# A one-core decoder layer with gathered experts: front stages in other slots, eight mixer weight buffers, and the v gather ahead of the u gather

## The chip, the cores and the metric
The kernel runs on one NeuronCore of one Trainium2 chip. The metric is the device time of one execution in microseconds (us); lower is better. Before the change it is 3838.55 us, the median of three runs (3834.42 to 3840.43).

## The reference, cut to what matters
One layer over 1024 tokens of width 1024, all in float32:

```python
z = rms_norm(h) @ w_in                       # 14 tiles RWKV-7, 8 tiles convolution, 16 tiles of gates, 128 columns each
o_r = rwkv7_branch(...)                      # recurrence over tokens, 8 heads of 64, then @ w_o (512 -> 1024)
o_c = conformer_conv_branch(...)             # 31 taps on 512 channels, layer norm, silu, then @ w_o (512 -> 1024)
h = h + (g_r * o_r + g_c * o_c) @ w_out      # sigmoid gates
# product-key experts: 8 heads x 16 experts per token = 128 rows of u_tab and of v_tab per token
...
        u = jnp.take(u_tab, ib, axis=0)
        coef = gb * jax.nn.gelu(jnp.einsum('cd,ced->ce', xb, u), approximate=False)
        return jnp.einsum('ce,ced->cd', coef, jnp.take(v_tab, ib, axis=0))
...
h = h + ple_gate * (p[i] @ ple_w_proj[i]); return rms_norm(h, final_norm_g)
```

Each token needs 128 rows of 4 KB from each of the two tables, so that the kernel gathers 1.07 GB.

## The kernel before, in words
The tokens are worked in 8 tiles of 128 (`NT`). For a tile the expert stage is cut in 128 **slots** (`SLOTS`). In a slot, GpSimd asks with one indirect DMA for one row of `u_tab` for each of the 128 tokens (tile `e_u`, or `e_a_rstd`, which serves as the fifth u buffer; `UR` = 5), and VectorE takes its dot product with the normed tokens `e_c` (line L1878 in the profile). Two tiles later (`LAG` = 2) GpSimd asks in the slots for rows of `v_tab` (tile `e_v`, `VR` = 6 buffers, line L745; the u rows are line L728), and TensorE adds one to the sum in PSUM `e_acc` with weights `e_wd` (L1051).

The main loop runs over **blocks** t = 0 to 10. Block t holds the u gathers and dots of tile t, the v gathers and additions of tile t-2, and spread over the same slots the **front** of tile t+1: everything from the projection to the first indices of the experts. The order of work on each engine is this written-out slot order; the engines are tied to each other only by semaphores, and each engine, SyncE's queue of DMA issues and GpSimd's too, works strictly in its own order. The front of tile 0 runs ahead of block 0 together with the first part of the projection (the **prologue**, 0 to 289 us).

The front in slots: 0 to 16 the preparation of the RWKV inputs (VectorE, ScalarE, some TensorE), 20 to 64 the 30 recurrence steps of TensorE, ScalarE and VectorE in turn (L770 to L856, results through `e_arena`, operands in `e_zb`), 0 to 65 the convolution's taps on VectorE (`e_gbc` from `e_hc`, L1617 for the first tap and L1620), from `MIX_AT` = 66 the norms, from 74 the eight conv products and from 80 the eight y products (`mixer_product`, L875), each with a 256 KB weight tile that SyncE loads into one of four buffers `e_ring` (L490), then the gating, `w_out` (L950), the residual, the query projection `e_w_q` (L967), the scores and the first two heads' top-k. The top-k of a head is 8 `head` stages and 6 `select` stages on VectorE, one a slot (L1782 to L1837); heads 2 to 7 follow in the slots of the block itself. From slot 84 on VectorE also does the first 44 taps of the next tile (`early_taps_at`), for which SyncE loads `e_hc` (L473).

Blocks 0 and 1 have no v gathers. In them TensorE does the projection of the last 768 tokens instead (**behind products**, L1121, 304 in each block, spread evenly by `behind_products` over slots 2 or 4 to 123), with weights that SyncE loads two tiles ahead.

What sets the order around the change are these lines:

```python
def ring_loads_at(s):
    return [k for k in range(2 * KT) if s == (40 + k if k < RING else product_slot(k - RING))]
...
                if s == EARLY_AT and n + 1 < NT:      # EARLY_AT = 84
                    conv_load(n + 1)
```

A ring load beyond the first four waits on SyncE for the product that frees its buffer (`s_wu`), and `conv_load` stands behind the last of them.

## Time and profile before

| | |
|---|---|
| median of three runs | 3838.55 us |
| the profiled execution's own time | 3844.25 us |
| its span, first to last instruction | 3842.0 us |
| TensorE busy | 2784.5 us (72%) |
| VectorE busy | 2356.3 us (61%) |
| GpSimd busy | 1981.9 us (52%) |
| software DMA queue (gathers), share of the 16 engines' span | 75.4% |
| blocks 0 and 1 | 341.5 and 339.2 us |
| blocks 2 to 6 | 423.5, 413.6, 414.3, 413.2 and 412.1 us |

The profiled execution is 5.7 us over the median of the runs, within their usual scatter of 0.3%. The lengths of the blocks go from first dot to first dot. A busy share is an average over stages with different limits, so the stages are read apart. In block 5 slot 64 begins at 2425.5 us, slot 72 at 2457.7, slot 80 at 2487.0, slot 96 at 2540.5; in block 6 slot 80 begins at 2903.4 us and slot 96 at 2948.5; in block 0 slots 24, 72 and 112 begin at 358.1, 480.8 and 596.0 us (the starts of the dots on VectorE).

### The profile page before, as it was taken

What the parts mean: (1) busy time and instruction counts of PE and PEld (TensorE: products, weight loads), DVE (VectorE), ACT (ScalarE), POOL (GpSimd) and SP (SyncE); (2) the same over time, 40 slices, a digit from 0 to 9 for tenths busy, and PEclk for the clock granted to TensorE, in tenths of its full rate; (3) what the DMA queues carried; (4) which work ended last, traced back from release to release, by engine and by line L of the source; (5) the groups of instructions that cost most, each with busy time, mean ns of one, the idle gap of its engine ahead of it and who ended that gap; (6) DMA issues with size and microseconds to landing.
All of it is one profiled execution on the core that took longest, in us unless ns stands there. A gap on an engine that the chain in (4) does not pass through costs nothing. (4 is left out here: it accounts for less than half of the span.)

```text
span 3842.0 us, 41409 instructions
## 1 busy us (share of the span) xinstructions
PE 2784.5 (72%) x15264; PEld 1299.4 (34%) x15264; DVE 2356.3 (61%) x6063; ACT 521.8 (14%) x1147; POOL 1981.9 (52%) x2093
## 2 busy tenths in 40 slices
PE   9977988999556765676566755775666687778777
PEld 7764655565123312232133312331222222111111
DVE  4549968977766686756766686657675666520000
ACT  3222212211111010101101011101010011100000
POOL 0003333333555565556555665556556666666663
PEclk9988998999677877887778867787678787779999
DMA  5538988898989999899989998999889999999995
GB/s 189 187 142 262 311 311 303 297 323 287 344 307 339 360 384 327 313 354 374 358 310 334 380 368 313 346 352 372 319 313 390 410 389 370 366 387 345 378 345 216
DMA packets 383386, 1255.86 MB, mean 327 GB/s; under 512 B 40400, under 2 KB 78544, under 8 KB 382544
## 3 DMA queue, kind: packets, MB, share of 16 engines
q0 software_dynamic: 294912, 1073.87, 75.4%
q1 hardware_dynamic: 83920, 177.25, 13.0%
q8 instruction: 120, 1.97, 0.2%
q10 hardware_dynamic: 4352, 2.10, 0.2%
q14 instruction: 82, 0.67, 0.0%
HBM read 1222.52 MB, written 30.54 MB: 326 GB/s over the span
## 5 line engine op out<-in xcount | busy, mean ns | idle before, releaser
L1051 PE MATMUL e_acc<-e_v,e_wd 128*32 128x512 f32 x3636 | 1079.8, 756 | 398.5 <-DMA e_v<-in_v_tab,e_idxT 271.3
L728 POOL DMA_INDIRECT e_u<-in_u_tab,e_idx x820 | 793.5, 968 | 1045.9 <-DVE e_dots L1878 577.1
L745 POOL DMA_INDIRECT e_v<-in_v_tab,e_idxT x909 | 872.9, 960 | 522.9 <-issue 224.2
L1878 DVE CUSTOM_DVE_ANT_0 e_u<-e_u,e_c 128x1024 f32<-128x1024 f32 x820 | 994.7, 1214 | 194.1 <-DMA e_u<-in_u_tab,e_idx 142.6
L1051 PEld LDWEIGHTS e_acc<-e_v,e_wd 128*32 128x32 f32 x3636 | 148.0, 120 | 983.7 <-DMA e_v<-in_v_tab,e_idxT 558.7
L1121 PE MATMUL e_acc<-e_v 128*128 128x384 f32 x1216 | 440.7, 508 | 18.9 <-DMA e_v<-in_w_in 12.2
L1620 DVE SCALAR_TENSOR_TENSOR e_gbc<-e_hc,e_cw,e_gbc 128x128 f32<-128x128 f32 x960 | 310.6, 345 | 1.9 <-remote 0.6
L770 PE MATMUL e_pd<-e_arena 64*64 64x64 f32 x3584 | 166.6, 249 | 188.5 <-ACT e_arena L1179 141.2
L728 POOL DMA_INDIRECT e_a_rstd<-in_u_tab,e_idx x204 | 197.9, 970 | 174.2 <-DVE e_dots L1878 131.2
L1121 PEld LDWEIGHTS e_acc<-e_v 128*128 128x128 f32 x1216 | 227.8, 196 | 173.0 <-issue 27.7
L1878 DVE CUSTOM_DVE_ANT_0 e_a_rstd<-e_a_rstd,e_c 128x1024 f32<-128x1024 f32 x204 | 247.6, 1214 | 44.4 <-DMA e_a_rstd<-in_u_tab,e_idx 34.0
L770 PEld LDWEIGHTS e_pd<-e_arena 64*64 64x64 f32 x3584 | 142.5, 159 | 331.7 <-ACT e_arena L1179 202.2
L1179 ACT ACTIVATE e_arena<-e_pd 128x512 f32<-128x512 f32 (+1 forms) x192 | 90.3, 470 | 780.3 <-remote 408.4
L1887 DVE TENSOR_TENSOR e_hh<-e_hh,e_acc 64x512 f32<-64x512 f32 (+1 forms) x24 | 16.5, 686 | 276.5 <-PE e_acc L1051 273.7
L950 PE MATMUL e_pd<-e_w_out,e_actT 128*128 128x512 f32 x256 | 132.5, 648 | 41.4 <-issue 37.4
L967 PEld LDWEIGHTS e_pd<-e_actT,e_w_q 128*128 128x128 f32 x1024 | 134.2, 210 | 56.4 <-issue 43.4
L967 PE MATMUL e_pd<-e_actT,e_w_q 128*128 128x128 f32 x1024 | 143.4, 299 | 9.7 <-ACT e_actT L1227 5.2
L1095 PE MATMUL e_acc<-e_w_q,e_u 128*128 128x256 f32 x608 | 144.1, 392 | 3.4 <-DVE e_w_q L1962 3.4
L1051 PE MATMUL e_acc<-e_u,e_wd 128*32 128x512 f32 x368 | 121.3, 613 | 25.0 <-DMA e_u<-in_v_tab,e_idxT 17.2
L1020 PE MATMUL e_pd<-e_w_out,e_actT 128*128 128x512 f32 x256 | 126.9, 631 | 6.6 <-issue 4.4
L1095 PEld LDWEIGHTS e_acc<-e_w_q,e_u 128*128 128x128 f32 x608 | 116.5, 195 | 23.6 <-issue 5.2
L875 PE MATMUL e_pd<-e_y,e_ring 128*128 128x128 f32 x512 | 84.3, 326 | 54.0 <-DMA e_ring<-in_w_r 50.7
(259 smaller groups left out, 2802.4 us busy)
## 6 DMA issues: line engine op xcount, KB each, us to landing
e_v<-in_w_in SPq DMA_DIRECT2D x76, 512.0 KB
e_u<-in_w_in SPq DMA_DIRECT2D x38, 512.0 KB, 3.9
e_ring<-in_w_c SPq DMA_DIRECT2D x64, 256.0 KB
e_ring<-in_w_r SPq DMA_DIRECT2D x64, 256.0 KB
e_v<-in_v_tab,e_idxT POOLq DMA_INDIRECT x909
e_u<-in_u_tab,e_idx POOLq DMA_INDIRECT x820
e_gt<-mixer_gates SPq DMA_DIRECT2D x16, 512.0 KB
e_arena<-shifted_projection SPq DMA_DIRECT2D x7, 896.0 KB
```

The source lines that it names most:

```text
L728: pool.indirect_dma_start(out=u[m % UR][:, :], out_offset=None, in_=io["u_tab"], in_offset=bass.IndirectOffsetOnAxis(ap=idx[n % 2][:, j:j ...
L745: pool.indirect_dma_start(out=v[i], out_offset=None, in_=io["v_tab"], in_offset=bass.IndirectOffsetOnAxis(ap=idxT[n % (LAG + 1)][:, k:k + ...
L770: last = pe.matmul(pi[r, out, i * CH:(i + 1) * CH], a[r, i, :], b[r, i, :] if len(b.shape) == 3 else b[r, :], start=True, stop=True)
L950: last = pe.matmul(pd[:, h * HALF:(h + 1) * HALF], mixt[:, k, :], w_out[:, k, h * HALF:(h + 1) * HALF], start=(k == 0), stop=(k == KT - 1))
L967: last = pe.matmul(pd[:, h * P:(h + 1) * P], w_q[:, k, h * P:(h + 1) * P], actT[:, k, :], start=(k == 0), stop=(k == KT - 1))
L1020: last = pe.matmul(pd[:, h * HALF:(h + 1) * HALF], actT[:, k, :], w_ple[:, k, h * HALF:(h + 1) * HALF], start=(k == 0), stop=(k == KT - 1))
L1051: last = pe.matmul(acc[rows, cols], w[:, at_:at_ + 32], v[v_place(m)[0]][:, cols], start=(step == 0), stop=True, skip_group_check=True)
L1095: last = pe.matmul(out, w_a[m % UW][:, k, :], ahead[:, k, :], start=(k == 0), stop=(k == KT - 1))
L1121: last = pe.matmul(acc[:, m % 2 * HALF:m % 2 * HALF + BEHIND_T], w_b[m % 2][:, k, :], behind[:, k, :], start=(k == 0), stop=(k == KT - 1))
L1179: act.activation(dst, src, ACT.Copy).then_inc(s_ra, 1)
L1620: dve.scalar_tensor_tensor(out=out, in0=hc[:, i, j:j + P], scalar=col(cw, j * CONV_TILES + i), in1=out, op0=ALU.mult, op1=ALU.add).then_in ...
L1878: dve.tensor_tensor_reduce(u[m % UR][:, :], u[m % UR][:, :], c[:, :], 1.0, 0.0, ALU.mult, ALU.add, dots[n % 2][:, j:j + 1]).then_inc(s_dot, 1)
```

## The change
It does six things:

1. Four more ring buffers (`RINGS` = 8). They are parts of `e_zb`, which lies idle between the end of a tile's recurrence and the next tile's preparation. Weight tiles 4 to 7 are now loaded at slots 66 to 69, behind a wait for the end of the recurrence, and tile k from 8 on at the slot of product k-8.
2. `conv_load` moves from slot 84 to slot 70 (for tile 1, in the prologue, ahead of slot 74).
3. The stages behind the y products move by one to three slots: y products 81 to 84, `w_out` from slot 90, the queries from 104, the first head's top-k from slot 109. Heads 2 to 7 start 3 slots later, so the last three `head` stages of head 1 fall into slots 0 to 2 of the next block instead of the end of the last. The early taps of tile 1, in the prologue, go to slots 102 to 107, 8 a slot.
4. The behind products of blocks 0 and 1 get weights: 1 in slots 74 to 113 (`HEAVY`), 3 elsewhere.
5. In the prologue tile 0's gates go straight from the projection into `e_gt` and `e_hh` instead of through memory, and `e_w_q` (4 MB) is loaded in two parts.
6. GpSimd asks in each slot first for the v row and then for the u row.

```diff
-UR, UW, VR, RING = 5, 4, 6, 4
+UR, UW, VR, RING, RINGS = 5, 4, 6, 4, 8
-HEAD_AT, HEAD_SPAN = 6, 14
+HEAD_AT, HEAD_SPAN = 9, 14
-NEXT_HEAD_AT = MIX_AT + 40
+NEXT_HEAD_AT = MIX_AT + 43
+HEAVY = (MIX_AT + 8, MIX_AT + 48)
-    first, each = (EARLY_AT + 6, 5) if t == 1 else (EARLY_AT, 1)
+    first, each = (MIX_AT + 36, 8) if t == 1 else (EARLY_AT, 1)
...
+def behind_weight(t, s):
+
+    if not BEHIND_AT[t] <= s < BEHIND_END:
+        return 0
+    return 1 if HEAVY[0] <= s < HEAVY[1] else 3
+
+
 def behind_products(t, s):
 
-    a, n, slots = s - BEHIND_AT[t], COL_TILES * KT, BEHIND_END - BEHIND_AT[t]
-    return range(n * a // slots, n * (a + 1) // slots) if 0 <= a < slots else range(0)
+    done, total = (sum(behind_weight(t, i) for i in range(n)) for n in (s, SLOTS))
+    n = COL_TILES * KT
+    return range(n * done // total, n * (done + behind_weight(t, s)) // total)
...
+def ring_slot(n, k):
+
+    if k < RING:
+        return 40 + k
+    if k < RINGS:
+        return MIX_AT + k - RING if n else FRONT_SLOTS
+    return product_slot(k - RINGS)
...
             def ring_load(n, which, m):
-                k = (2 * n + which) * KT + m
-                if k >= RING:
-                    sp.wait_ge(s_wu, k - RING + 1)
+                k = which * KT + m
+                if k >= RINGS:
+                    sp.wait_ge(s_wu, 2 * KT * n + k - RINGS + 1)
+                elif k >= RING:
+                    sp.wait_ge(s_rp, REC_PE * 2 * (n + 1))
...
-                if s == EARLY_AT and n + 1 < NT:
+                if n and n + 1 < NT and s == MIX_AT + 4:
                     conv_load(n + 1)
...
             for t in range(NT + LAG):
                 for j in range(NSEL):
+                    if t >= LAG:
+                        gather_v(t - LAG, j)
                     if t < NT:
                         gather_u(t, j)
-                    if t >= LAG:
-                        gather_v(t - LAG, j)
...
-                        if s < 6:
-                            select(t, 1, s)
+                        if 0 <= s - head_slot(1) - 8 < 6:
+                            select(t, 1, s - head_slot(1) - 8)
+                        if s < head_slot(1) + 8:
+                            head(t, 1, s - head_slot(1))
```

SyncE's queue in block 2, where it loads for the front of tile 3 (`e_ring` and `e_zb` the weight buffers, `e_hc` the convolution's inputs, `e_arena` the next tile's RWKV inputs), before:

```order
L483 DMA e_gt<-mixer_gates 128x1024
L490 DMA e_ring<-in_w_c 128x512 x8
L490 DMA e_ring<-in_w_r 128x512 x4
L483 DMA e_gt<-mixer_gates 128x1024
L490 DMA e_ring<-in_w_r 128x512 x2
L468 DMA e_arena<-shifted_projection 128x1792
L490 DMA e_ring<-in_w_r 128x512 x2
L473 DMA e_hc<-conv_input 128x4x158
L505 DMA h_after_mixer<-e_x 128x1024
```

The same place in the changed kernel:

```order
L510 DMA e_gt<-mixer_gates 128x1024
L522 DMA e_ring<-in_w_c 128x512 x4
L522 DMA e_zb<-in_w_c 128x512 x4
L502 DMA e_hc<-conv_input 128x4x158
L522 DMA e_ring<-in_w_r 128x512 x4
L522 DMA e_zb<-in_w_r 128x512 x4
L510 DMA e_gt<-mixer_gates 128x1024
L497 DMA e_arena<-shifted_projection 128x1792
L537 DMA h_after_mixer<-e_x 128x1024
```

The `e_hc` load has moved from behind all eight y weight tiles and the 0.9 MB `e_arena` load to ahead of them.

TensorE in block 0 around the mixer products of tile 1 (L875, later L908), with the behind products (`e_acc<-e_v`) between them, before:

```order
L1121 MATMUL e_acc<-e_v 128x384 x5
L875 MATMUL e_pd<-e_gbc,e_ring 128x128 x8
L1121 MATMUL e_acc<-e_v 128x384 x3
L875 MATMUL e_pd<-e_gbc,e_ring 128x128 x8
L1121 MATMUL e_acc<-e_v 128x384 x2
L875 MATMUL e_pd<-e_gbc,e_ring 128x128 x8
L1121 MATMUL e_acc<-e_v 128x384 x3
L875 MATMUL e_pd<-e_gbc,e_ring 128x128 x8
L1121 MATMUL e_acc<-e_v 128x384 x7
L875 MATMUL e_pd<-e_y,e_ring 128x128 x8
```

And in the changed kernel:

```order
L1155 MATMUL e_acc<-e_v 128x384 x14
L908 MATMUL e_pd<-e_gbc,e_ring 128x128 x8
L1155 MATMUL e_acc<-e_v 128x384
L1023 MATMUL e_ps<-e_keys,e_qT 128x128 x2
L908 MATMUL e_pd<-e_gbc,e_ring 128x128 x8
L1155 MATMUL e_acc<-e_v 128x384
L908 MATMUL e_pd<-e_gbc,e_zb 128x128 x8
L1155 MATMUL e_acc<-e_v 128x384
L908 MATMUL e_pd<-e_gbc,e_zb 128x128 x8
L1155 MATMUL e_acc<-e_v 128x384 x5
L908 MATMUL e_pd<-e_y,e_ring 128x128 x8
```

One behind product stands now between two slots of mixer products, where two or three stood; more of them stand ahead.

## Rows read from the trace of the kernel before

**Rows 1.** Busy time by stage: prologue, block 0, block 4, block 7
```profile
core 0: us, PE busy (x) PEld busy (x) DVE busy (x) ACT busy (x) POOL busy (x), PEclk, DMA share, GB/s
0.00:289.00 289.00, 254.93 (x1770) 206.97 (x1771) 138.37 (x399) 71.65 (x146) 13.48 (x48) 0.95 0.52 173
289.00:630.00 341.00, 302.51 (x1701) 190.36 (x1699) 287.31 (x759) 68.30 (x143) 125.47 (x127) 0.93 0.85 293
...
1807.00:2221.00 414.00, 264.23 (x1626) 113.94 (x1626) 283.15 (x734) 44.29 (x101) 247.81 (x256) 0.77 0.93 347
...
3046.00:3460.00 414.00, 302.78 (x903) 76.32 (x907) 224.37 (x514) 60.68 (x133) 271.34 (x281) 0.79 0.99 380
```

**Rows 2.** Waits of GpSimd in block 4 (total, times, longest)
```profile
POOL e_u L728 <- DVE e_dots L1878: 52.9, 19, 12.6
...
POOL e_v L745 <- PE e_acc L1051: 16.7, 12, 4.5
```

**Rows 3.** GpSimd in order of time, two places in block 4
```profile
2088.64 0.94 POOL L745 DMA_INDIRECT e_v<-in_v_tab,e_idxT  x1 [0.80 <-PE e_acc L1051]
2102.19 0.94 POOL L728 DMA_INDIRECT e_u<-in_u_tab,e_idx  x1 [12.61 <-DVE e_dots L1878]
...
2188.95 0.93 POOL L728 DMA_INDIRECT e_u<-in_u_tab,e_idx  x1 [0.30 <-issue]
...
2191.43 0.94 POOL L728 DMA_INDIRECT e_u<-in_u_tab,e_idx  x1 [0.30 <-issue]
```

**Rows 4.** The `e_hc` load: its users, its time to landing, one issue
```profile
L1617 DVE TENSOR_SCALAR e_gbc<-e_hc,e_cw,e_vec 128x128 f32<-128x128 f32 x32 | 10.5, 343 | 101.2 <-DMA e_hc<-conv_input 86.9 <-PE e_pd L875 14.3
...
DMA to landing us min/median/max: 11.7/13.8/16.4
...
2085.81 0.38 SPq L473 DMA_DIRECT2D e_hc<-conv_input  x1
```

**Rows 5.** Busy time: block 5 slots 64, 80, 96 on; block 6 slots 80, 96 on
```profile
2425.00:2487.00 62.00, 45.40 (x234) 21.30 (x234) 39.57 (x100) 9.89 (x22) 34.84 (x36) 0.75 0.95 356
2487.00:2541.00 54.00, 35.57 (x145) 15.75 (x144) 29.73 (x70) 0.72 (x2) 29.26 (x31) 0.81 0.91 339
2541.00:2617.00 76.00, 56.68 (x268) 25.16 (x266) 50.68 (x133) 6.36 (x18) 50.06 (x53) 0.80 0.98 370
...
2903.00:2949.00 46.00, 38.59 (x157) 16.36 (x157) 27.61 (x59) 1.39 (x4) 28.55 (x31) 0.92 1.01 399
2949.00:3034.00 85.00, 53.29 (x254) 22.78 (x252) 43.88 (x105) 6.10 (x17) 53.84 (x57) 0.79 1.01 399
```

**Rows 6.** Waits of TensorE in block 4
```profile
PE e_pd L770 <- ACT e_arena L1179: 27.1, 5, 8.2
...
PE e_pd L875 <- DMA e_ring<-in_w_r: 10.1, 4, 4.4
```

**Rows 7.** Busy time in block 0: slots 0, 24 and 72 on
```profile
290.00:358.00 68.00, 48.65 (x165) 28.01 (x164) 67.60 (x179) 15.63 (x36) 24.78 (x24) 0.78 0.78 252
358.00:481.00 123.00, 120.46 (x978) 75.11 (x977) 112.37 (x307) 32.03 (x69) 45.66 (x49) 1.00 0.90 305
481.00:596.00 115.00, 100.46 (x422) 66.03 (x421) 76.61 (x193) 17.40 (x33) 39.54 (x41) 0.93 0.83 294
```

**Rows 8.** The behind products alone (L1121), block 0 slots 24 to 71
```profile
358.00:481.00 123.00, 90.23 (x254) 45.22 (x253) 1.00 0.90 305
```

**Rows 9.** VectorE: stages 5 to 7 of a head (prologue); block 4 slots 8 on
```profile
275.51 0.09 DVE L1806 MATCH_VALUE_LOAD e_pos<-e_best,e_onehot 128x8 f32 x1
...
277.42 0.25 DVE L1820 TENSOR_SCALAR e_half<-e_pos 128x16 uint32<-128x16 uint32 x2
...
1832.50:1858.40 25.90, 16.06 (x44) 2.74 (x46) 25.77 (x61) 4.47 (x7) 17.02 (x18) 0.70 1.03 408
```

**Rows 10.** Prologue: TensorE's wait for y weights; VectorE's early taps and first top-k
```profile
PE e_pd L875 <- DMA e_ring<-in_w_r: 2.9, 2, 2.0
...
249.77 8.22 DVE L1620 SCALAR_TENSOR_TENSOR e_gbc<-e_hc,e_cw,e_gbc 128x128 f32<-128x128 f32 x31
...
271.77 0.49 DVE L1782 MAX8 e_tv<-e_sc 128x8 f32<-128x128 f32 x2 [8.57 <-ACT e_sc L1361]
```

More of the change, by code:

```diff
@@ L303, in trunk @@
         gbc, hc = buf("e_gbc", [P, 3, PAIRS, P]), buf("e_hc", [P, CONV_TILES, PADT + P])
+        flat_zb = zb[:, :, :, :, :, :].rearrange("p c w i a t -> p (c w i a t)")
+        ring += [flat_zb[:, i * PAIRS * P:(i + 1) * PAIRS * P].rearrange("p (i t) -> p i t", i=PAIRS) for i in range(RINGS - RING)]
         arena = buf("e_arena", [P, 34 * P])
@@ L389, in trunk @@
         s_const, s_iota = sem("e_constants"), sem("e_iota_made")
-        s_w_q, s_w_tail = sem("e_query_weights_in"), sem("e_tail_weights_in")
-        s_ident, s_vec, s_up, s_x = sem("e_identity_made"), sem("e_vectors_in"), sem("e_up_weights_in"), [sem(f"e_xT_in{i}") for i in range(KT)]
+        s_w_q, s_w_tail = [sem(f"e_query_weights_in{i}") for i in range(2)], sem("e_tail_weights_in")
+        s_ident, s_vec, s_up, s_x = sem("e_identity_made"), sem("e_vectors_in"), sem("e_up_weights_in"), [sem(f"e_xT_pair_in{i}") for i in range(KT // 2)]
         s_asq, s_asum, s_avar, s_arstd = sem("a_x_squared"), sem("a_squares_summed"), sem("a_variance_inverted"), sem("a_rstd_ready")
@@ L409, in trunk @@
         s_rp, s_ra, s_rv = sem("e_rec_step_in_psum"), sem("e_rec_copied"), sem("e_rec_combined")
-        s_gin, s_ring = sem("e_mixer_gate_in"), [sem(f"e_mixer_weights_in{i}") for i in range(RING)]
+        s_gin, s_ring = sem("e_mixer_gate_in"), [sem(f"e_mixer_weights_in{i}") for i in range(RINGS)]
         s_wu, s_cg = sem("e_mixer_weights_used"), sem("e_conv_gated")
@@ L486, in ring_load @@
             def ring_load(n, which, m):
-                k = (2 * n + which) * KT + m
-                if k >= RING:
-                    sp.wait_ge(s_wu, k - RING + 1)
-                sp.dma_start(ring[k % RING][:, :, :], io[("w_c", "w_r")[which]][m]).then_inc(s_ring[k % RING], 16)
+                k = which * KT + m
[3 more added lines that the diff above has]
+                    sp.wait_ge(s_rp, REC_PE * 2 * (n + 1))
+                elif n:
+                    sp.wait_ge(s_wu, 2 * KT * (n - 1) + k + RINGS + 1)
+                i = ring_turn(n, k)[0]
+                sp.dma_start(ring[i][:, :, :], io[("w_c", "w_r")[which]][m]).then_inc(s_ring[i], 16)
             def gain_load(n):
@@ L540, in front @@
                     x_load(n)
-                if s == 30:
+                if n and s == 30:
                     gate_load(n, 0)
-                for k in ring_loads_at(s):
+                for k in ring_loads_at(n, s):
                     ring_load(n, k // KT, k % KT)
-                if s == MIX_AT + 12:
+                if n and s == MIX_AT + 13:
                     gate_load(n, 1)
-                if s == EARLY_AT and n + 1 < NT:
+                if n and n + 1 < NT and s == MIX_AT + 4:
                     conv_load(n + 1)
-                if s == MIX_AT + 34:
+                if s == MIX_AT + 36:
                     h_store(n)
@@ L593, in _ @@
             for k in range(KT):
-                sp.dma_start(ahead[:, k, :], io["xT"][k][:, 0:AHEAD_T]).then_inc(s_x[k], 16)
+                sp.dma_start(ahead[:, k, :], io["xT"][k][:, 0:AHEAD_T]).then_inc(s_x[k // 2], 16)
             sp.dma_start(vec[:, :], io["vec"]).then_inc(s_vec, 16)
@@ L619, in _ @@
                 for s in front_slots(p):
-                    for k in ring_loads_at(s):
+                    for k in ring_loads_at(0, s):
                         ring_load(0, 0, k)
@@ L623, in _ @@
                 behind_w(0, m)
-            gate_load(0, 0)
+            conv_load(1)
+            sp.wait_ge(s_am, COL_TILES)
+            sp.wait_ge(s_late, 16)
+            sp.dma_start(w_q[:, 0:W_Q_FIRST, :], io["w_q"][:, 0:W_Q_FIRST, :]).then_inc(s_w_q[0], 16)
             for s in range(FRONT_SLOTS, SLOTS):
@@ L871, in mixer_product @@
             def mixer_product(n, which, m, x):
-                k = (2 * n + which) * KT + m
-                pe.wait_ge(s_ring[k % RING], 16 * (k // RING + 1))
+                at_, turn = ring_turn(n, which * KT + m)
+                pe.wait_ge(s_ring[at_], 16 * turn)
                 for i in range(PAIRS):
-                    last = pe.matmul(pd[:, m * P:(m + 1) * P], ring[k % RING][:, i, :], x[:, i, :],
+                    last = pe.matmul(pd[:, m * P:(m + 1) * P], ring[at_][:, i, :], x[:, i, :],
                                      start=(i == 0), stop=(i == PAIRS - 1))
```

95 lines of the change are left out of this document (55 added, 40 removed).

## The prediction, made before the changed kernel had run
> **What bounds the kernel now.** I read the stages first, since a share over the whole span mixes them [rows 1]. In block 7, where no front runs, the DMA engines are busy 0.99 of the time at 380 GB/s; in block 4 it is 0.93 at 347 GB/s, in block 0 0.85 at 293 GB/s with TensorE busy 302.5 of 341 us. So blocks 0 and 1 are TensorE's, and blocks 2 to 6 are the transfers' with holes. The holes come from GpSimd standing still. When nothing holds it, a u gather follows the last after 2191.43 - 2188.95 = 2.48 us, 1.24 us a gather [rows 3]; 256 gathers would take 317 us of a block's 414. The rest is waits, above all for a u buffer that a dot must free: 52.9 us in 19 waits in block 4, against 16.7 us for v buffers freed by TensorE [rows 2].
>
> The longest of these waits, 12.6 us, has one cause in each block. SyncE issues the `e_hc` load at 2085.81 behind the last y weight tile, the load takes 11.7 to 16.4 us to land, and the first tap stands in front of the dots on VectorE: 101.2 us of idle VectorE in seven waits [rows 4], 5.2 of them in the prologue, 14 in each of blocks 0 and 1, about 17 in each of blocks 2 to 5. While VectorE waits, five u buffers fill, GpSimd blocks on the sixth, and the v gather behind it blocks too [rows 3].
>
> **hc load at slot 70.** It is issued behind the end of the recurrence and the last tap of the tile (slots 64 to 66), and used at slot 84: some 18 slots at over 3 us against a landing of 16.4 at most. The wait goes entirely. What the block gets back is less than 17 us, for the DMA engines work through most of the stall. Block 6 has no tile 8 to load for, so it is the kernel's own test: slots 80 to 95 take 46 us there, 54 in block 5, at 399 against 339 GB/s [rows 5]. That is 8 us. Lower bound: the engines' idle share, 0.09 of 54 us, 4.9 us. Upper bound: the GpSimd stall, 12.6 us. I take 8 us for each of blocks 2 to 5, **-32 us**. What is late next is the transfers themselves: block 6 then runs at DMA share 1.01.
>
> **Ring buffers.** TensorE waits 10.1 us in block 4 for y weights [rows 6], but that time lies just ahead of and inside the e_hc stall; without it the wait would still hold v additions up. With eight buffers the y tiles are asked for seven slots ahead of use instead of two to four, and these waits end too; they are in the 8 us above, for block 6 has only part of them. New is that 4 tiles, 1.05 MB, move from slots 74 and 75 to 66 to 69, where the engines run at 356 GB/s of the 399 they can [rows 5]. In a full stretch 1.05 MB cost 2.6 us at 399 GB/s; bounds 0 and 2.6 us, I take 1.6 for five blocks, **-8 us**.
>
> What SyncE is made to wait for at slot 66, the end of the recurrence, has passed by then; behind it stand the `e_hc` load, the y tiles and in blocks 0 and 1 the next behind weights, which are asked for a tile ahead. The Trainium skill, "DMA: Bandwidth & Descriptors", section on queues, rings and completion order, says that each engine goes round robin between queues packet by packet, so that SyncE's loads take a share of their own beside the gathers. The trace agrees, as far as an e_hc load of 0.3 MB with some 2.5 MB ahead of it lands in 13.8 us (median), about half of 399 GB/s. By that rule the y tiles asked for together at slots 74 to 77 slow the gathers there rather than wait for them.
>
> **Head 1's last three stages** move to slots 0 to 2 of blocks 0 to 6. Stages 5 to 7 take 277.42 - 275.51 = 1.9 us, and VectorE is full there: 67.6 of 68 us in block 0 [rows 7], 25.77 of 25.9 in block 4 [rows 9]. The time leaves the end of the block, where VectorE has room. Bounds 0 and 1.9 us a block, that is 0 to 13; **+10 us**, since the recurrence follows on VectorE at once.
>
> **Behind products.** One costs 90.23 us / 127 (two records each) = 0.71 us [rows 8]. Before, a slot had 304/122 = 2.5; now 304 x 3/286 = 3.2 outside slots 74 to 113 and 1.06 inside. In block 0:
> - slots 2 to 23: +15 products, 11 us, under VectorE's full 67.6 us with TensorE idle 19 [rows 7]: 0.
> - slots 24 to 71: 48 x 0.7 = 34 products more, 24 us, and TensorE is busy 120.5 of 123 us: +22 us (its idle 2.5 taken).
> - slots 72 to 111: 38 x 1.43 = 54 less, plus 1 more ahead: 38 us of TensorE's 100.5 in 115 [rows 7]. VectorE is busy 76.6 there, which bounds the stretch from below: it can lose 0 to 38 us. The chain through products, gates, `w_out` and queries stays; with TensorE's remaining 63 us, some waits of either on the other and a granted clock that falls under the 0.93 of now, I put it at 90 us: -25 us. Slots 84's 14 us of VectorE are in it.
> - slots 112 to 123: +3 to 4 products net, +3 us.
> Sum 0 for block 0 and the same for block 1, bounds -13 and +25 each: **0 us**.
>
> **Prologue.** The y products lose 2.9 us of waits for weights. The early taps (8.22 us for 31, so 12 us for 44) stood between the two halves of the residual; now they stand behind it, in the 8.57 us in which VectorE waits for the scores [rows 10], and overrun that by about 3. Three stages of head 1 leave. Between 0 and 8 us; **-5 us**. The two parts of `e_w_q` and the gates that no longer pass through memory (2 MB less) lie in stretches where the engines are half idle (0.52, [rows 1]): nothing; if they weren't covered, 2 MB are 5 us more.
>
> **v before u.** The order stays alternating; what changes is that GpSimd, blocked on u, has issued one v more, and blocked on v one u less. Upper bound per block 19 x 1.24 = 24 us won against 12 x 1.24 = 15 lost [rows 2, 3], 9 us net, 43 for five blocks. But many of the waits lie in the recurrence, where TensorE waits for ScalarE (27.1 us, [rows 6]) and not for rows; there an earlier v row wins nothing. At the start of block 2, u gather 0 now waits behind the end of the behind products, about +3 us. Together **-2 us**.
>
> **Sum.** -32 - 8 + 10 + 0 - 5 - 2 = -37 us, from the profiled execution's 3844 to 3807 us. That execution stands 5.7 us over the median of the runs, so against these 3838.55 - 37 = 3802 us.
>
> **Rivals.**
> - *The transfers take most of it* (0.13): only the 4.9 us of idle engines per stall come back and the ring's move gives nothing: -20 + 10 - 5 - 2 = -17, 3822 us. For it: DMA share 0.98 in slots 96 on of block 5 already. Against it: block 6, 399 GB/s against 370 there [rows 5].
> - *TensorE pays in blocks 0 and 1* (0.12, the other side): the extra 34 products in slots 24 to 71 cost 22 us each time, and the stretch of slots 72 to 111 doesn't give them back since its chain and the clock hold it. Were it to shrink by nothing, 2 x 25 - 37 = +13, 3852 us. From a shrinkage below 25 - 37/2 = 6.5 us per block on it decides. For it: TensorE full at clock 1.00 in slots 24 to 71. Against it: VectorE idle 38 us in the stretch.
> - *The mixer stretch falls to VectorE's floor* (0.12): 77 us instead of 90: 2 x 13 = 26 us more, 3776 us.
> - *The v order wins* (0.10): 9 us in each of blocks 2 to 6 as bounded above, 3802 - 41 = 3761 us. For it: u waits outnumber v waits 19 to 12.
> - *A stall only moves* (0.05): the y tiles' burst at slots 74 to 77 delays u rows as much as the e_hc wait did; then -5 + 10, within 0.2%.
>
> **How the numbers follow.** The forecast has 0.48, with a range of its own of 3784 to 3822 us (the bounds 4.9 to 12.6 us of the stall term alone give 12 up and 18 down). Over all cases 3764 to 3842 us: below it lies most of the v order's case, above it TensorE's. A measurement of this kernel can tell about 0.2%, 7.7 us. Faster by more: 0.48 + 0.13 + 0.12 + 0.10 less the near ends of the first two, 0.82; within 0.2%: 0.07; slower: 0.11.
>
> **What would show each step.** The waits of the first tap for `e_hc` and of the mixer products for their weights should be near zero, and no GpSimd wait above 6 us should stand near slot 90. Slots 80 to 95 of blocks 2 to 5 should take about 46 us at near 399 GB/s, these blocks about 405 us, block 6 about 411. In block 0 slots 24 to 71 should take about 145 us and slots 72 to 111 about 90; the sum tells the second rival from the third. The first dot should come near 284 us. What would make me wrong: recurrence slots that change in length, on which I put nothing although heads and gathers shift against them, or the behind products.

## The result and the profile after

The changed kernel takes 3708.41 us in the median of four runs (3703.92 to 3718.76), the kernel before 3839.49 us beside it (four runs, 3834.42 to 3857.01). The ratio is 0.9655, with a 95% interval of 0.9618 to 0.9692. The prediction was 3802 us with a range of 3764 to 3842: the gain is 131 us where 37 were forecast, and the time lies below the range. The profiled execution has a span of 3704.3 us, 137.7 less than before. Two executions of the same kernel differ too: the trace of the kernel before that was taken in a later session (before_again) is 31.7 us shorter than this one, and its slots 0 to 15 and 112 to 127 differ by 3.0 and 2.5 us in the mean of blocks 2 to 5. Differences of one stage below some 3 us are therefore not read as effects here.

Busy time by stage in the changed kernel: prologue, block 0, block 4 and block 7, to be read against [rows 1]. The columns are the window, then busy time and instructions of each engine, the granted clock, the DMA engines' share and GB/s.

```profile
core 0: us, PE busy (x) PEld busy (x) DVE busy (x) ACT busy (x) POOL busy (x), PEclk, DMA share, GB/s
0.00:278.00 278.00, 247.39 (x1768) 200.75 (x1769) 137.66 (x392) 72.47 (x162) 12.23 (x47) 0.97 0.51 168
278.00:611.00 333.00, 296.91 (x1698) 185.76 (x1696) 288.99 (x763) 69.88 (x144) 126.61 (x130) 0.96 0.89 307
1743.00:2128.00 385.00, 261.90 (x1626) 111.07 (x1626) 284.68 (x733) 44.42 (x101) 242.70 (x253) 0.77 0.97 367
2916.00:3284.00 368.00, 263.98 (x778) 64.45 (x778) 222.76 (x514) 50.71 (x112) 241.07 (x254) 0.77 0.99 382
```

The work of the engines is nearly the same, block 4 is 29 us shorter, and its transfers run at 367 GB/s instead of 347. From first dot to first dot (starts of the dots on VectorE), the 137.7 us split up so, in us:

| stretch | before | after | change |
|---|---|---|---|
| prologue | 290.2 | 278.2 | -12.0 |
| block 0 | 341.5 | 332.6 | -8.9 |
| block 1 | 339.2 | 346.0 | +6.8 |
| blocks 2 to 5 together | 1664.6 | 1568.0 | -96.6 |
| block 6 | 412.1 | 390.8 | -21.3 |
| block 7 and the tail | 794.5 | 788.7 | -5.8 |

Inside blocks 2 to 5 (mean of one block) slots 0 to 15 went from 51.8 to 52.7 us, **slots 16 to 63 from 155.5 to 146.2**, slots 64 to 71 from 32.6 to 32.7, slots 72 to 83 from 36.0 to 35.2, **slots 84 to 95 from 46.0 to 31.3**, and slots 96 to 127 from 94.2 to 94.0. For slots 16 to 63 nothing was foreseen. The 8 us foreseen were for slots 80 to 95, and these fell by 6.3 (53.3 to 47.0). But the y products now begin in slot 81 and not in 80, so that neither stretch holds the same work as before. Slots 72 to 95 together do: they fell from 82.1 to 66.5 us, 15.6 less, where stall and ring buffers were forecast at 8 and 1.6.

GpSimd's waits in block 4 of the changed kernel (total, times, longest), against [rows 2], followed by the row of the kernel before that [rows 2] leave out:

```profile
POOL e_v L778 <- remote: 35.1, 21, 3.4
POOL e_v L778 <- PE e_acc L1085: 30.4, 23, 5.2
...
POOL e_u L761 <- DVE e_dots L1924: 14.8, 16, 2.5
```

```profile
POOL e_v L745 <- remote: 26.1, 18, 2.8
```

The u waits fell from 52.9 to 14.8 us, and none of these waits is over 5.2 us. The v waits rose from 16.7 to 30.4 us; beside them stand waits whose releaser the profile can't name ("remote"; 26.1 us before, 35.1 after). This program runs on one core, so no other core can be the releaser: the profile found no instruction that ended just before the wait did. That row is the one that I had passed over.

Block 5 from slots 64, 80 and 96 on, and block 6 from slot 80 on, against [rows 5]:

```profile
2329.00:2381.00 52.00, 38.90 (x225) 18.00 (x224) 38.88 (x93) 8.66 (x19) 33.08 (x35) 0.91 1.00 383
2381.00:2428.00 47.00, 33.08 (x131) 13.78 (x132) 31.70 (x80) 1.93 (x4) 29.54 (x32) 0.82 1.03 409
2428.00:2525.00 97.00, 68.25 (x300) 26.36 (x298) 62.53 (x160) 6.37 (x18) 65.83 (x68) 0.81 1.00 383
2770.00:2816.00 46.00, 34.88 (x138) 13.45 (x131) 29.45 (x69) 1.93 (x4) 30.43 (x32) 0.81 1.03 407
```

Slots 80 to 95 take 47 us at 409 GB/s; 46 us at 399 GB/s were forecast from block 6. Block 0 from slots 0, 24 and 72 on, against [rows 7]:

```profile
278.00:348.00 70.00, 53.94 (x198) 30.92 (x197) 67.71 (x174) 18.15 (x42) 25.80 (x26) 0.91 0.83 280
348.00:490.00 142.00, 139.88 (x1036) 86.57 (x1035) 113.98 (x314) 30.88 (x66) 46.26 (x49) 1.00 0.88 293
490.00:579.00 89.00, 76.32 (x364) 51.91 (x363) 75.51 (x188) 17.60 (x30) 38.18 (x41) 0.92 0.92 332
```

142 and 89 us, where 145 and 90 were forecast. The behind products alone in slots 24 to 71 (L1155), against [rows 8]:

```profile
348.00:490.00 142.00, 110.46 (x316) 56.82 (x315) 1.00 0.88 293
```

### The profile page after: what moved, and what is told of

Same layout as the page of the kernel before. It is cut to its first block, busy times and chain, and to the rows that moved or that the text cites. A ratio compares the mean times of both kernels' runs of the same rounds, so it can differ in the third digit from the quotient of the medians.

```text
span 3704.3 us, 41438 instructions
## 1 busy us (share of the span) xinstructions
PE 2755.3 (74%) x15264; PEld 1272.2 (34%) x15264; DVE 2368.4 (64%) x6063; ACT 525.3 (14%) x1165; POOL 1979.5 (53%) x2093
## 4 chain that ended last, share of the span: by engine, by line
PE 19%; DVE 18%; another core or an unknown queue 15%; issue 11%; DMA 10%; POOL 8%; ACT 2%; SPq 0%; POOLq 0%; DVEq 0%; ACTq 0%
DVE e_u L1924 6%; PE e_acc L1085 6%; DMA e_v<-in_v_tab,e_idxT 5%; POOL e_v L778 4%; DMA e_u<-in_u_tab,e_idx 3%; PE e_pd L983 2%; PE e_acc L1155 2%; POOL e_u L761 2%; DVE e_gbc L1659 2%; PE e_pd L1001 2%; PE e_pd L803 2%; DVE e_a_rstd L1924 2%; PE e_pd L1054 2%; PE e_pd L908 1%
## 5 line engine op out<-in xcount | busy, mean ns | idle before, releaser
L1155 PE MATMUL e_acc<-e_v 128*128 128x384 f32 x1216 | 434.3, 501 | 24.7 <-DMA e_v<-in_w_in 16.6
L1155 PEld LDWEIGHTS e_acc<-e_v 128*128 128x128 f32 x1216 | 224.7, 193 | 178.2 <-issue 28.6
L983 PE MATMUL e_pd<-e_w_out,e_actT 128*128 128x512 f32 x256 | 138.2, 671 | 35.4 <-DVE e_actT L1790 26.7
L778 POOL DMA_INDIRECT e_u<-in_v_tab,e_idxT x92 | 86.7, 943 | 48.9 <-issue 23.7
```

Source lines behind the costliest of these rows:

```text
L778: pool.indirect_dma_start(out=v[i], out_offset=None, in_=io["v_tab"], in_offset=bass.IndirectOffsetOnAxis(ap=idxT[n % (LAG + 1)][:, k:k + ...
L983: last = pe.matmul(pd[:, h * HALF:(h + 1) * HALF], mixt[:, k, :], w_out[:, k, h * HALF:(h + 1) * HALF], start=(k == 0), stop=(k == KT - 1))
L1155: last = pe.matmul(acc[:, m % 2 * HALF:m % 2 * HALF + BEHIND_T], w_b[m % 2][:, k, :], behind[:, k, :], start=(k == 0), stop=(k == KT - 1))
```

## The experiments

All times are medians; each ratio is to the kernel before, run in the same session. The ratio on record is not exactly the quotient of the two medians, so both are given where they differ. The sessions fell in two groups, and this turned out to be the main thing. In the one the kernel before takes 3809 to 3846 us, in the other 3513 to 3515 us. I call them the first and the second kind of chip. The record numbers the chips 5 and 4 in sessions of the first kind and 4, 8 and 2 in those of the second. Number 4 stands in both, and whether it names the same chip there is not known, so the "kind" may be a property of a chip or a state that a chip was in at the time. The result above and all of [rows 1 to 10] are of the first kind.

### The order of the two gathers alone
The kernel before with one edit (before_v_first, and again in another session as v_first_again), and the changed kernel with the order turned back (after_u_first):

```diff
                 for j in range(NSEL):
+                    if t >= LAG:
+                        gather_v(t - LAG, j)
                     if t < NT:
                         gather_u(t, j)
-                    if t >= LAG:
-                        gather_v(t - LAG, j)
```

> The kernel before with only the gather order changed (v row first). Order theory: 30 to 45 us faster than before (some 3800 us), in slots 16 to 63 of blocks 2 to 6. Stall theory: within 10 us of before, since the e_hc stall is untouched. The prediction's own term was 2 us.

> The changed kernel with one thing undone: GpSimd asks again for the u row first, then for the v row. Order theory: the v row asked for before GpSimd stands still for a u buffer is what shortens slots 16 to 63 of blocks 2 to 6 by some 8 us each, so this kernel loses about 40 us against the changed one (some 3750 us), slots 16 to 63 go back to about 155 us, and slots 72 to 95 stay near 66 us. Stall theory: the gain is the e_hc stall alone, so the time stays within 10 us of 3708 us.

> The kernel before with the v row first. Theory 1, the order pays only against late signals: within 8 us of the kernel before where they are absent, 60 to 80 us faster where they are there. Theory 2, in the kernel before the order also lets v rows pass the stall of the first tap: 10 to 25 us faster without late signals too.

Measured: 0.9816 [0.978, 0.9852] (3768.02 against 3845.74 us), and 0.9822 [0.9782, 0.9862] (3749.69 against 3808.94). The changed kernel with u first has 0.9798 [0.9764, 0.9831], 3761.0 us, where the changed kernel has 0.9655. So on this kind of chip the order is worth 59 to 78 us in the kernel before by the medians, 68 to 71 by the ratios, more than the 30 to 45 expected. In the changed one it is, by the two ratios, 0.0143 x 3846 = 55 us. These two ratios come from different sessions, and their intervals together leave 36 to 74 us. Recurrence slots 16 to 63 and slots 84 to 95 of block 4 with the order alone (before they take 155 us at 316 GB/s and 45 us at 351 GB/s):

```profile
1827.00:1974.00 147.00, 91.62 (x872) 45.76 (x872) 104.73 (x292) 13.25 (x31) 87.19 (x92) 0.73 0.93 337
2041.00:2082.00 41.00, 24.50 (x87) 9.32 (x86) 23.39 (x52) 0.31 (x1) 21.05 (x22) 0.75 0.97 361
```

And GpSimd's waits in that block 4, to be read against [rows 2]:

```profile
POOL e_v L745 <- PE e_acc L1051: 39.0, 27, 7.6
...
POOL e_u L728 <- DVE e_dots L1878: 18.8, 17, 3.2
```

The u waits fell by 34 us and the v waits rose by 22. The transfers are what changed: the share of the DMA engines in slots 16 to 63 rose to 0.93. In blocks 2 to 5 the mean gain is 17.6 us, 8.4 of it in slots 16 to 63 and 5.4 in slots 84 to 95; in the second session (v_first_again beside before_again) it is 14.7, 8.1 and 6.3. In the changed kernel the order gives 9.3 us a block (after beside after_u_first), so its gain and those of the other parts overlap.

### The early e_hc load alone
before_hc_early and hc_early_again, one line of SyncE in the kernel before:

```diff
-                if s == EARLY_AT and n + 1 < NT:
+                if n + 1 < NT and s == (MIX_AT + 4 if n >= 2 else EARLY_AT):
                     conv_load(n + 1)
```

> The kernel before with only the e_hc load moved from slot 84 to slot 70, for tiles 3 to 7 (loads of blocks 1 to 5; tiles 1 and 2 as before). Stall theory: slots 80 to 95 of blocks 2 to 5 go from 54 to about 46 us or less and the kernel gains 8 to 16 us for each of these four blocks, and up to 14 us in block 1: 35 to 70 us. Prediction's term: 32 us in blocks 2 to 5. If the wait only moves to the ring loads, the gain is under 15 us and TensorE's waits for weights grow.

> The kernel before with the e_hc load of tiles 3 to 7 at slot 70. Theory 1, the prediction's term: slots 84 to 95 of blocks 2 to 5 fall by 8 us each, and without late signals nothing gives it back, 25 to 35 us faster. Theory 2, transfers take it back as where it was measured first: 10 to 20 us faster.

Measured: 0.9954 [0.9933, 0.9974] and 0.9934 [0.9905, 0.9964], 18 and 25 us. The waits for `e_hc` (VectorE) and for the weights (TensorE) over the whole kernel:

```profile
DVE e_gbc L1617 <- DMA e_hc<-conv_input: 19.4, 2, 14.0
...
PE e_pd L875 <- DMA e_ring<-in_w_r: 45.8, 23, 7.0
PE e_pd L875 <- DMA e_ring<-in_w_c: 29.1, 15, 4.7
```

The first was 86.9 us in six waits [rows 4] and is gone but for tiles 1 and 2, whose load was left in place; TensorE's stay. Block 4 from slot 84 and from slot 96 on:

```profile
2071.00:2108.00 37.00, 28.10 (x104) 11.46 (x105) 23.77 (x55) 0.31 (x1) 22.50 (x24) 0.86 0.99 381
2108.00:2207.00 99.00, 67.19 (x286) 24.89 (x284) 62.95 (x162) 6.37 (x18) 64.22 (x67) 0.78 0.98 375
```

Slots 84 to 95 lost 8.9 us in the mean of blocks 2 to 5 (46.0 to 37.1; 8.6 in the second session), the forecast 8. But the blocks lost only 4.8 us, in both sessions, less than the 8 to 16 that the expectation had. Where the rest is given back is not settled: in the first session slots 0 to 15, 96 to 111 and 112 to 127 grew by 2.4, 2.2 and 1.1 us, in the second slots 72 to 83, 96 to 111 and 112 to 127 by 1.4, 1.1 and 2.6, while slots 0 to 15 fell by 1.5. Each of these is within what two traces of one kernel differ by.

### Eight weight buffers alone
before_eight_rings and rings_again: the kernel before with the ring of the change, its loads at slots 66 to 69 and product k-8; the `e_hc` load still at slot 84.

```diff
-UR, UW, VR, RING = 5, 4, 6, 4
+UR, UW, VR, RING, RINGS = 5, 4, 6, 4, 8
-    return [k for k in range(2 * KT) if s == (40 + k if k < RING else product_slot(k - RING))]
+    if k < RING:
+        return 40 + k
+    if k < RINGS:
+        return MIX_AT + k - RING if n else FRONT_SLOTS
+    return product_slot(k - RINGS)
```

> The kernel before with only the four more weight buffers (tiles 4 to 7 loaded at slots 66 to 69, tiles 8 on at the slot of product k-8; the e_hc load still at slot 84; the semaphores of the first x loads are paired to make room for four more). Ring theory: TensorE's waits for weights go, 79 us in all, and with them the e_hc load is issued some 10 us earlier, so that the e_hc wait of 17 us shrinks too: 20 to 50 us gained. Stall theory in its narrow form: the e_hc load stands still behind the eight tiles and the 0.9 MB load, so under 15 us.

> The kernel before with eight weight buffers, the e_hc load still at slot 84. Theory 1, the weights' waits and a part of the stall were one and the same time: 15 to 30 us faster without late signals, less than the 45 us where they are. Theory 2, the eight buffers are slack against late signals alone: within 8 us.

Measured: 0.9883 [0.9847, 0.992] and 0.9851 [0.9811, 0.9892], 45 and 57 us by the ratios, 53 and 48 by the medians. VectorE's wait for `e_hc` over the whole kernel:

```profile
DVE e_gbc L1641 <- DMA e_hc<-conv_input: 67.6, 7, 11.4
```

No wait of TensorE for a weight tile is left, and the wait for `e_hc` fell too, from 86.9 us in six waits and 14.3 in a seventh put down to TensorE [rows 4] to 67.6 in seven, since SyncE no longer stands behind the y tiles. Slots 84 to 95 take 38.6 us against 46.0, 7.4 less, and the blocks 10.7 less (10.0 in the second session). Do stall and ring, two terms of my sum, lie over the same time? Over the whole block they hardly do: alone they give 4.8 and 10.7 us, and with both and the other parts of the change except the order (after_u_first) the block is 14.9 us shorter. In slots 72 to 95 it is 8.6 and 8.8 alone, 15.5 together.

### The other parts, and two steps further
after_even_behind gives blocks 0 and 1 back the even spread; after_slots_back puts y products, `w_out`, queries and heads back; after_v_ahead (again: v_ahead_again) asks in slot j for v row j+1; after_adds_last (again: adds_last_again) lets TensorE add the v row behind the front's work of the slot.

```diff
 # after_even_behind (it has the e_hc load of block 0 at slot 78, too)
-    return range(n * done // total, n * (done + behind_weight(t, s)) // total)
+    return range(n * a // slots, n * (a + 1) // slots) if 0 <= a < slots else range(0)
 # after_slots_back (and fifteen like it)
-HEAD_AT, HEAD_SPAN = 9, 14
+HEAD_AT, HEAD_SPAN = 6, 14
-NEXT_HEAD_AT = MIX_AT + 43
+NEXT_HEAD_AT = MIX_AT + 40
 # after_v_ahead
-                        gather_v(t - LAG, j)
+                        for i in range(j + (j > 0), min(j + 2, NSEL)):
+                            gather_v(t - LAG, i)
 # after_adds_last, in TensorE's slot
-                            add_tokens(t - LAG, s, together)
...
                         front(t + 1, s)
+                            add_tokens(t - LAG, s, together)
```

> The changed kernel with the behind products of blocks 0 and 1 spread evenly again (and, so that TensorE has freed what it needs, the e_hc load of block 0 at slot 78). Theory 1, the prediction's term of 0: slots 24 to 71 of block 0 fall from 142 us to about 120, slots 72 to 111 rise from 89 to about 111, blocks 0 and 1 as long as now within 5 us, about 3708 us. Theory 2, the weights gave block 0 the 9 us it lost: blocks 0 and 1 are 9 us longer each, about 3726 us. Theory 3, the weights cost block 1 its 7 us: block 1 is 339 us again and the kernel faster than 3702 us.

> The changed kernel with y products, w_out, queries and heads back in the slots of before (the last three stages of head 1 in slots 123 to 125 again); eight rings, the early e_hc load, the v row first and the weights of the behind products stay. Theory 1, the prediction's term: the head's stages in slots 0 to 2 cost 1.4 us in each of 7 blocks, so this kernel is about 10 us faster, 3698 us, with slots 0 to 15 of blocks 2 to 5 at 51.3 us instead of 52.7. Theory 2, the shift costs nothing, since the blocks are transfer-bound: 3708 within 8 us. Theory 3, the shift keeps y products away from their weights: slots 84 to 95 of blocks 2 to 5 go from 31.3 us up by 2 to 4 us, in all about 3720 us.

> The changed kernel with GpSimd asking in slot j for v row j+1 and then for u row j, another slot further in the direction of the change. Theory 1, what counts is that GpSimd never stands at one table's full buffers while a buffer of the other is free: GpSimd already waits longer for v buffers (65 us in block 4) than for u buffers (15 us), so a further slot tips the balance; the waits for v grow, u rows come late, and the kernel is slower by 10 to 40 us, 3718 to 3748 us. Theory 2, TensorE gets its v rows in time because they are asked for earlier: another slot gives a part of the 52 us again, 3670 to 3700 us, and TensorE's waits for e_v in block 4 fall from 26 us to under 18.

> The changed kernel with TensorE adding the v row of a slot behind the front's work of that slot, not ahead of it, so that a late v row holds no recurrence step or product of the same slot, and v buffers come free a part of a slot later. Theory 1, buffers in flight decide: nothing won, 0 to 20 us slower, 3708 to 3728 us, with GpSimd's waits for v buffers in block 4 over 70 us. Theory 2, late v rows in front of the recurrence decide: slots 16 to 63 of blocks 2 to 5 fall from 146 us by 3 to 8 us, in all 3670 to 3695 us.

All four ran on the second kind of chip, where the kernel before takes 3514.78 us. Measured: 0.9945 [0.9925, 0.9966], 0.9944 [0.9922, 0.9965], 0.9981 [0.9971, 0.9991] and 0.995 [0.9933, 0.9968]. The numbers in the expectations were for the first kind, so they can't be compared directly with these. The next session had the changed kernel itself on the second kind, with the order of the gathers and two of the four again:

> The changed kernel as it is, once more, because the runs so far came from chips that differ: where the kernel before takes 3846 us, TensorE's last matmul of a step is signalled 2 to 8 us late some 400 times in blocks 2 to 6, and where it takes 3515 us never. Theory 1, the gain of the change comes mostly from slack against these late signals: with the late signals the ratio is again 0.96 to 0.97, without them 0.993 to 0.997. Theory 2, the gain does not depend on them: the ratio is 0.96 to 0.97 either way.

> The changed kernel with the u row first again. Theory 1, the order pays by slack against late signals: with them 40 to 60 us slower than the changed kernel beside it, without them within 8 us of it. Theory 2, the order pays by rows in flight alone: 40 to 60 us slower either way.

> The changed kernel with v row j+1 asked for ahead of u row j. Theory 1, slack for TensorE: with late signals TensorE's v rows have another slot, 10 to 30 us faster than the changed kernel beside it; without them GpSimd's waits for v buffers only hold the u rows, 5 to 15 us slower. Theory 2, balance of the two tables: 10 to 40 us slower either way.

> The changed kernel with the addition of a slot's v row behind the front's work of that slot. Theory 1, v rows in front of the recurrence cost little since they wait for TensorE and not it for them (they lie landed for 9 to 12 us in slots 24 to 63): within 10 us of the changed kernel beside it. Theory 2, late v rows hold the recurrence: 15 to 40 us faster.

| beside the kernel before at 3514.23 us | ratio | us |
|---|---|---|
| changed kernel (after_again) | 0.9903 [0.9879, 0.9928] | 3482.07 |
| with u first (u_first_again) | 0.9905 [0.9877, 0.9932] | 3481.66 |
| v row j+1 ahead of u row j (v_ahead_again) | 0.9974 [0.9964, 0.9985] | 3505.85 |
| additions last in the slot (adds_last_again) | 0.9938 [0.9916, 0.996] | 3494.8 |

Here the change gains 32 us and not 131, and no gain of the order is seen (0.4 us the other way, the intervals leave 13 either way). The ratio of 0.9903 is a little below the 0.993 to 0.997 expected. Another slot of lead for v costs 24 us, later additions 13. The next two differences are between sessions. Taking the weights of the behind products back costs (0.9945 - 0.9903) x 3514 = 15 us, with intervals that leave 4 to 26. In the traces block 0 takes 346.2 us instead of 332.0 and block 1 351.3 instead of 341.7, but the profiled execution of after_even_behind is itself 12 us over its median. Taking the slots back costs 14 us by the ratios (3 to 26), though the profiled spans differ by only 6.0, of which 4.1 lie in the prologue. Whether v rows asked for earlier still, or later additions, would pay on the first kind of chip wasn't measured, nor whether the weights and the slots pay there.

Last, the kernel before on the first kind again, then on the second, and the three parts (order, `e_hc` for tiles 3 to 7, eight rings) together in the kernel before:

> The kernel before as it is, for its stages beside the next three. Theory 1 (late signals stretch the recurrence): where they are absent, slots 16 to 63 of blocks 2 to 5 take 120 to 130 us instead of 155, slots 84 to 95 take 40 to 46 us as before, and the kernel about 3515 us. Theory 2: all stages are shorter in proportion, 9%.

> The kernel before as it is. Without late signals: slots 16 to 63 of blocks 2 to 5 take 120 to 130 us instead of 155, slots 84 to 95 some 38 to 42 us against 31.6 in the changed kernel. With them: the lengths of before_again within 3 us in each stage.

> The kernel before with eight weight buffers, the early e_hc load (tiles 3 to 7) and the v row first together; slots, behind products and prologue as before. With late signals: if the three gains added up, 18 + 50 + 65 = 133 us less; they overlap where the change itself came to 131, so I expect 95 to 115 us less than the kernel before, ratio 0.970 to 0.975, and the rest from the prologue and block 0. Without late signals: theory 1, the three are worth the prediction's stall and rings, 15 to 25 us less, ratio 0.993 to 0.996, the prologue the rest of the change's 32; theory 2, they are worth nothing and it is all prologue and blocks 0 and 1.

before_again has a ratio of 0.9999 [0.9976, 1.0022], before_third 0.9995 [0.9985, 1.0004], 1 to 2 in a thousand being what such a comparison can't tell. rings_hc_v_all fell on the second kind: 0.9953 [0.9937, 0.9969], 16 us less. The profiled spans differ by 8.2 us only.

### What differs between the two kinds of chip
Slots 16 to 63, 64 to 71 and 72 to 95 of block 4 of the kernel before on the second kind (before_third):

```profile
1734.00:1858.00 124.00, 90.46 (x910) 38.70 (x910) 107.20 (x294) 15.06 (x37) 92.03 (x97) 0.90 1.03 409
1858.00:1881.00 23.00, 14.82 (x92) 5.14 (x91) 21.02 (x48) 3.75 (x9) 14.38 (x16) 1.00 1.03 409
1881.00:1955.00 74.00, 54.26 (x235) 23.43 (x233) 47.75 (x117) 5.33 (x10) 45.28 (x47) 0.82 1.01 390
```

The recurrence stretch takes 124 us at 409 GB/s with the DMA engines busy throughout (share 1.03), where it took 155 us at 316 GB/s and a share of 0.88. So the transfers bound it on the second kind, with and without the change (in after_again 123 us, 409 GB/s, share 1.03). ScalarE's waits show what else differs. The three longest of the kernel before on the first kind, whole kernel:

```profile
ACT e_wd L1387 <- PE e_acc L1051: 440.3, 21, 34.4
ACT e_arena L1179 <- remote: 408.4, 50, 13.6
ACT e_wd L1387 <- remote: 252.8, 9, 38.4
```

and of the same kernel on the second (before_third), where no wait of any engine has an unnamed releaser:

```profile
ACT e_wd L1387 <- PE e_acc L1051: 593.8, 31, 40.8
ACT e_sc L1361 <- PE e_ps L989: 363.2, 54, 25.3
ACT e_arena L1179 <- PE e_pd L770: 354.7, 108, 10.8
```

On the second kind it is TensorE that ends these waits. On the first it is TensorE too, but late. One place of many, in order of time, in block 4 of the changed kernel on the first kind:

```profile
1846.66 0.63 PE L803 MATMUL e_pd<-e_m_id,e_arena 64*64 64x64 f32 x16
...
1847.23 1.06 PE L1085 MATMUL e_acc<-e_v,e_wd 128*32 128x512 f32 x8
...
1854.04 0.60 ACT L1213 ACTIVATE e_arena<-e_pd 128x512 f32<-128x512 f32 x1 [7.30 <-remote]
1854.34 0.94 POOL L778 DMA_INDIRECT e_v<-in_v_tab,e_idxT  x1 [1.70 <-remote]
...
1854.69 1.12 PE L803 MATMUL e_pd<-e_arena 64*64 64x64 f32 x16 [6.40 <-ACT e_arena L1213]
```

TensorE's step ends by its rows at 1847.3 us, the additions at 1848.3. ScalarE, which waits for that step alone, and GpSimd, which waits for the additions, both go on only at 1854.0 and 1854.3. In the trace's semaphore events the two signals come together, at 1854.02 and 1854.08 us. The same step on the second kind (after_slots_back):

```profile
1760.39 0.63 PE L803 MATMUL e_pd<-e_m_id,e_arena 64*64 64x64 f32 x16
...
1761.07 0.60 ACT L1213 ACTIVATE e_arena<-e_pd 128x512 f32<-128x512 f32 x1 [1.46 <-PE e_pd L803]
```

ScalarE starts 0.05 us after the product's end. To count such places I took from the trace's semaphore events how long after a matmul's end the next event on its semaphore came. The expectations speak of some 400 late ones, a count over all matmuls. That count is too high: on the first kind the events themselves are incomplete. The 1024 additions of v rows left 801 to 847 events there and 1026 on the second kind, and where an event is missing the next one is taken for a late one. The semaphore of the recurrence steps is nearly complete on both (247 to 254 and 252 to 258 events for 256 signals). Of its 160 signals in blocks 2 to 6, those over 2 us late (and under 20) were:

```
first kind:  before 79, before_again 65, before_v_first 86, v_first_again 83,
             before_hc_early 81, hc_early_again 67, before_eight_rings 74,
             rings_again 65, after_u_first 71, after 83
second kind: before_third 1, rings_hc_v_all 3, after_again 0, u_first_again 3,
             after_slots_back 0, after_even_behind 0, after_v_ahead 3,
             v_ahead_again 3, after_adds_last 2, adds_last_again 0
```

The count goes with the kind and not visibly with the kernel. In the kernel before on the first kind the 79 delays add up to 400 us, while its blocks 2 to 6 are 282 us longer than on the second (2076.7 against 1794.6). I call such a place a **halt**. Ends of matmuls are modelled, so whether TensorE stood still or its signal came late can't be told apart. A low granted clock does not single the halts out: in the changed kernel it is 1.00 from 1846.0 to 1848.3 us and 0.70 from there to 1854.0, but over all delays of the recurrence signals its mean is 0.82, against 0.77 over blocks 2 to 6.

## Why the prediction was wrong, point by point

**How far the order alone explains it.** The changed kernel with the u row first is 0.0202 x 3846 = 78 us faster than the kernel before, and the terms other than the order summed to -35. So of the 94 us between forecast and result some 53 are the order's and some 43 the other terms', the ring buffers' above all.

**The v order (-2 us): this step failed.** Alone it is worth 59 to 78 us, in the changed kernel 55. I had bounded it by 19 u waits x 1.24 = 24 us won less 12 v waits x 1.24 = 15 lost per block, and had then set even the 9 us aside, because TensorE waits for ScalarE in the recurrence "and not for rows; there an earlier v row wins nothing". Slots 16 to 63, that is the recurrence, gained 8.4 and 8.1 us a block by the order alone and 6.0 in the changed kernel. The blocks gained 17.6 and 14.7 us by the order alone, toward the won side of my bound; the changed kernel's 9.3 us a block come out at the rival "the v order wins", which had 9.

Why the order gains so much is in part argued. In a halt of TensorE the v buffers fill, then the u buffers, and what is in flight when GpSimd blocks is what the DMA engines have to work on. With v first it is more (share 0.93 instead of 0.88 in slots 16 to 63). A v wait costs less than I charged for it, which I argue from the sums and did not measure apart: GpSimd's waits in block 4, for dots, for TensorE and "remote" together, are 103 us before and 85 with the order alone. The second kind of chip fits: there are hardly any halts there, and the order is worth 0 in the changed kernel. GpSimd waits for u buffers there as well (32.4 us in block 4 of before_third), but the DMA engines are full throughout the recurrence, so that an earlier request can win nothing. But the two kinds differ in more than the halts, the order alone was not run on the second, and no run here takes the halts away and leaves the rest.

That part of ScalarE's and TensorE's waits were halts, I missed: I took the 27.1 us of [rows 6] as the recurrence's own chain. On the second kind the same row has 0.5 us.

**Ring buffers (-8 us): mis-sized.** The waits ended as foreseen (TensorE's waits for weights are 1.6 us in the whole changed kernel), but the size is 10 us a block in place of 1.6. I had counted the waits for weights as part of the stall's 8 us since they lie "just ahead of and inside" it, and they are a gain of their own: at the level of the block stall and buffers add up (4.8 and 10.7 alone, 14.9 together). The buffers also let SyncE reach the `e_hc` load earlier: that wait fell from 101.2 to 67.6 us with them alone. On the second kind rings, `e_hc` and order together are worth 16 us.

**e_hc stall (-32 us): right in place, too large in sum.** Its 8 us a block came out at 8.9 and 8.6 in slots 84 to 95 (9.2 and 9.6 in the slots 80 to 95 that it was forecast for), but the block gained 4.8 only; alone it gives 18 to 25 us. I had read from block 6 what the stretch gains, and not whether the block does. On the second kind slots 84 to 95 fall from 35.4 to 31.3 with all three parts, while slots 64 to 71, where the moved loads now lie, rise from 23.5 to 26.9. That is the rival "The transfers take most of it", and it fits this term. The moved loads are four weight tiles and the `e_hc` load, 1.37 MB, and at the 409 GB/s of those slots they take 3.4 us (an estimate). The Trainium skill, "DMA: Bandwidth & Descriptors", section on queues, rings and completion order, says that each engine goes round robin between its queues packet by packet. By that rule loads that move slow the gathers where they land; the 3.4 us agree, but they can't tell it from a service in order of arrival, since the engines are full there either way (share 1.03).

**Behind products (0 us): right in the stretches, and in the net as far as the runs tell.** 142 and 89 us against a forecast of 145 and 90. On the second kind blocks 0 and 1 together take 675.4 us with the even spread and the slots of before (rings_hc_v_all) and 673.7 in the changed kernel. The 15 us that the weights are worth are against an even spread beside the new slots of `w_out` and queries, which is worse than the kernel before was (slots 96 to 111 of block 0: 54.8 us, before 49.6). Block 1 lost at its end what the order costs there: the first v gather stands behind the last behind products, and the u rows behind it. GpSimd at that place in the changed kernel:

```profile
945.97 1.00 POOL L770 MEMSET e_wd<- 128x516 f32 x2 [10.33 <-PE e_acc L1155]
```

I had given this +3 us; slots 112 to 127 of block 1 went from 33.4 to 44.0 us, and are 34.9 with u first: the order costs about 9 us there.

**Head 1's stages (+10 us): too dear.** Slots 0 to 15 of blocks 2 to 5 grew by 0.9 us, and by 0.4 on the second kind with the shift against without; both are less than two traces of one kernel differ by. In sum the shift costs nothing on the second kind.

**Prologue (-5 us): mis-sized,** -12.0 and on the second kind -11.0. The first top-k there begins at 264.73 us instead of 271.77 [rows 10]:

```profile
264.73 0.48 DVE L1828 MAX8 e_tv<-e_sc 128x8 f32<-128x128 f32 x2
```

On the second kind the sum of 32 us is near the forecast's 37, but that is luck. In the profiled spans, which differ by 25 us, 11 are the prologue's and 10 block 0's, 5 are lost in block 1, and blocks 2 to 6, where order, rings and stall were to bring 42, bring 6. One slip in the working: the forecast's own range ended at 3822 us, but 12 up from 3802 is 3814. It changes nothing here, since the time lies below.

## What to carry to other kernels
Read the waits with an unnamed releaser before anything else: here, on one core, they were waits for an engine that the profile takes to be done. An order of requests that looks neutral can then be worth what it keeps in flight meanwhile. When a stall is removed, test the length of the whole block and not of the stretch, and compare stretches that hold the same work. Repeat the measurement in another session before you tune further: the same change was worth 131 us in one and 32 in another.

## What the runs showed of the hardware
In five sessions with numbered chips the kernel before took 3809 and 3846 us in two (the first kind) and 3513 to 3515 us in three (the second). Whether that belongs to the chip or to its state then is open, since number 4 stands in both groups. On the first kind 65 to 86 of the 160 recurrence signals of blocks 2 to 6 come over 2 us after the modelled end of their matmul, on the second 0 to 3. In the kernel before the mean granted clock is 0.823 and 0.829 on the first and 0.888 on the second; whether that is a cause or goes with it, and what halts TensorE, stays open. The DMA engines reach the same rate in both: 409 GB/s in slots 80 to 95 of block 5 of the changed kernel on the first kind, 409 in slots 16 to 63 of block 4 of the kernel before on the second.
